# A mixture-of-experts kernel on one core: experts ranked by their token count, three of the eight passes in fp32 column tiles, one pass for 160 tokens

## The reference, cut to what matters

```python
N_EXPERTS = 8; TOP_K = 2; EXPERT_DIM = 3584            # D_MODEL = 1024, 256 tokens
logits = (xf @ router_w).astype(jnp.float32)
top_val, top_idx = lax.top_k(logits, TOP_K)
gates = jax.nn.softmax(top_val, axis=-1)
...
def expert_block(args):
    tok_b, e = args
    return swiglu(x_pad[tok_b], w1[e], w3[e], w2[e])    # (silu(x w1) * (x w3)) w2
```

## Time and profile before

| what | value |
|---|---|
| median of three runs | 1640.24 us |
| profiled execution, first to last instruction (its span; no other time of that execution is given) | 1635.5 us |
| median less span | 4.7 us |
| TensorE busy | 1608.7 us, 98% of the span |
| VectorE busy | 1425.0 us, 87% |
| ScalarE busy | 1163.9 us, 71% |
| GpSimd busy | 69.7 us, 4% |
| DMA | 520.04 MB, mean 318 GB/s |
| weights of the experts | 189 slots of 2 MB: 168 issued by SyncE, 21 by ScalarE |
| mean granted TensorE clock | 0.999 |

### The profile page before, as it was taken

One profiled execution on the slowest core, in us unless ns is written; L12 is line 12 of the kernel. 1 busy time (PEld: TensorE's weight loads), 2 busy tenths in 40 slices (PEclk: granted clock), 3 DMA queues, 4 the chain that ended last, 5 costly groups with the idle time before them and its releaser, 6 DMA issues.

```text
span 1635.5 us, 21435 instructions
## 1 busy us (share of the span) xinstructions
PE 1608.7 (98%) x8554; PEld 1361.2 (83%) x8554; DVE 1425.0 (87%) x1628; ACT 1163.9 (71%) x1427; POOL 69.7 (4%) x53
## 2 busy tenths in 40 slices
PE   6999999999999999999999999999999999999998
PEld 4867899998897888888888888888888888888887
DVE  2579888888766999999998999998999998999997
ACT  3567544446556877888887888887888887888885
POOL 0000000000000000200200200200200200200200
PEclk9999999999999999999999999999999999999999
DMA  9956768877812998999998999999999999999992
GB/s 351 331 211 236 252 254 299 302 268 290 289 73 104 351 354 332 354 376 377 352 380 335 353 376 377 355 369 345 352 378 372 354 368 349 354 367 359 373 366 83
DMA packets 170323, 520.04 MB, mean 318 GB/s; under 512 B 6861, under 2 KB 9050, under 8 KB 170218
## 3 DMA queue, kind: packets, MB, share of 16 engines
q1 hardware_dynamic: 156736, 473.32, 77.5%
q10 hardware_dynamic: 13482, 45.29, 7.3%
HBM read 516.50 MB, written 2.10 MB: 317 GB/s over the span
## 4 chain that ended last, share of the span: by engine, by line
PE 81%; DVE 12%; DMA 3%; ACT 2%; issue 1%; ACTq 0%; DVEq 0%
PE bank L1335 20%; PE bank L1339 20%; PE bank L1338 20%; DVE ada_acc L1999 4%; DVE w_lo L2200 3%; DMA ring<-in_ffn_w 3%; PE bank L809 2%; PE bank L1349 2%; PE bank L772 2%; PE bank L766 2%; PE bank L1072 1%; PE bank L1266 1%; DVE w_lo L2491 1%; PE bank L1074 1%; PE bank L1075 1%
## 5 line engine op out<-in xcount | busy, mean ns | idle before, releaser
L2491 DVE TENSOR_TENSOR w_lo<-ring,w_hi 128x1024 fp32r<-128x1024 f32 x756 | 928.6, 1262 | 59.8 <-ACT w_hi L1801 37.4
L1801 ACT ACTIVATE w_hi<-ring 128x1024 fp32r<-128x1024 f32 x756 | 799.8, 1063 | 193.7 <-PE bank L1339 191.5
L1335 PE MATMUL bank<-w_hi,hg_hi 128*128 128x512 f32 x1008 | 394.0, 391 | 0.7 <-DVE hg_lo L2504 0.6
L1339 PE MATMUL bank<-w_hi,hg_lo 128*128 128x512 f32 x1008 | 392.5, 389 | 0.0
L1338 PE MATMUL bank<-w_lo,hg_hi 128*128 128x512 f32 x1008 | 392.3, 389 | 0.0
L1335 PEld LDWEIGHTS bank<-w_hi,hg_hi 128*128 128x128 f32 x1008 | 189.3, 188 | 40.2 <-DVE w_lo L2491 1.2
L1339 PEld LDWEIGHTS bank<-w_hi,hg_lo 128*128 128x128 f32 x1008 | 189.2, 188 | 39.4
L1338 PEld LDWEIGHTS bank<-w_lo,hg_hi 128*128 128x128 f32 x1008 | 189.3, 188 | 38.3
L1335 PE MATMUL bank<-w_hi,hid_hi 128*128 128x512 f32 x496 | 195.6, 394 | 0.0
L1339 PE MATMUL bank<-w_hi,hid_lo 128*128 128x512 f32 x496 | 193.4, 390 | 0.0
L1338 PE MATMUL bank<-w_lo,hid_hi 128*128 128x512 f32 x496 | 193.2, 389 | 0.0
(11 more groups left out here) (398 smaller groups left out, 2063.4 us busy)
## 6 DMA issues: line engine op xcount, KB each, us to landing
ring<-in_moe_w SPq DMA_DIRECT2D x168, 2048.0 KB, 8.2
ring<-in_ada_w SPq DMA_DIRECT2D x24, 2048.0 KB, 12.8
ring<-in_moe_w ACTq DMA_DIRECT2D x21, 2048.0 KB, 9.8
ring<-in_ffn_w SPq DMA_DIRECT2D x15, 2048.0 KB, 8.3
ring<-in_gla_w_in SPq DMA_DIRECT2D x6, 2048.0 KB, 12.8
ring<-in_da_w_in SPq DMA_DIRECT2D x4, 2048.0 KB, 12.5
ring<-in_da_w_in SPq DMA_DIRECT2D x4, 1024.0 KB, 17.2
ring<-in_da_w_out SPq DMA_DIRECT2D x2, 2048.0 KB, 10.6
```

Of the source, the lines that this page charges most:

```text
L1335: begun = mm(out[:, :], xhi, whi[:, cs], start=first, stop=False)
L1339: last = mm(out[:, :], xlo, whi[:, cs], start=False, stop=end)
L1801: A(w_hi[:, moe_slot(Q), :], raw_piece(m, q), ACT.Copy).then_inc(hi_done, 1)
L2491: v.tensor_tensor(w_lo[:, moe_slot(Q), :], raw_piece(m, q), w_hi[:, moe_slot(Q), :].bitcast(F32), ALU.subtract).then_inc(lo_done, 1)
```

## The change

**Ranking.** In pass 0, which always takes expert 0, VectorE ranks experts 1 to 7 by token count (`places`) and writes the expert of each later pass into `ovi`. SyncE reads these seven numbers into registers, one for each slot it issues from slot 14 of pass 0 on, and loads the weights of passes 1 to 7 from addresses given by register. Gates and positions are put in the order of the passes (`gate_m`, `pos_m`).

**Kinds of passes.** The eight passes have the kinds A B A A A B C B. By `PLACES`, pass 6 gets the expert with most tokens of the seven, passes 2, 3 and 4 ranks 1 to 3, passes 1, 5 and 7 ranks 4 to 6.

- A, 128 slots: as before.
- B, 64 slots (`light`): no splitting. The moving operand is the weight slot itself in fp32, the stationary operand 128x64 tokens in fp32 (`xb`). Two column groups of 64 work on the two halves of a slot's columns, so a slot takes 8 matmuls of 512 columns (16 of 256 in the last chunk), and a result of 64 tokens by 1024 columns lies in one bank. ScalarE and VectorE do only the SiLU, the product, the copies and the gather. A slot is released by its last matmul. The first pieces of the pass that follows are split only after the light pass's last step on ScalarE and VectorE.
- C, 128 + 32 slots: 128 tokens as in A; the further 32 in plain fp32 in four column groups of 32 (`further_up` after each w1 slot, using it and the w3 slot behind it, which is ordered next to it; `further_down` after each w2 slot), with their own transposes, gates and scatter.

**Overflow.** Passes for experts whose tokens exceed the capacity of their pass run after the end of all eight, behind branches only (`overflow`). The ninth pass is no longer begun in any case, and ScalarE issues no slots unless a branch is taken.

**The end.** Pass 7 is a light one; `out_end` waits for its last slot, scales both halves (64 partitions each), splits, scatters and adds. `last_by_halves` is gone.

The core of the diff:

```diff
+BASE = "ABAAABCB"
+KINDS = BASE + "A" * OVER
+PLACES = (NE - 1, 4, 1, 2, 3, 5, 0, 6)
+CAPS = {"A": P, "B": HALF, "C": P + XT}          # 128, 64, 160
...
-                    src, k, n = expert_source(m, i)
+                    src, k, n = expert_source(ids[m], KINDS[m], i)
                     sp.dma_start(slot_view(at, k, n), src).then_inc(landed[at % SLOTS], 16)
+                    if m == 0 and i >= PER - NE + 1:
+                        j = len(ids)
+                        sp.wait_ge(s_places, 1)
+                        ids.append(sp.value_load(ovi[0:1, j:j + 1], min_val=0, max_val=NE - 1))
...
+            def further_up(m, c, part):
...
+                for kk in range(n):
+                    k = 4 * part + kk
+                    for g in range(4):
+                        w = slot_view(at[g // 2], n, width)
+                        last = mm(psum[4][XT * g:XT * (g + 1), 0:hw], xc[:, k, :], w[:, kk, g % 2 * hw:(g % 2 + 1) * hw],
+                                  start=(k == 0), stop=(k == KT - 1))
+                last.then_inc(slot_left, 1)
...
+            def further_down(m, c, part):
...
+                for p in range(PPC):
...
+                    for half in range(2):
+                        g = 2 * half + p % 2
+                        last = mm(psum[5][XT * g:XT * (g + 1), :], hidx[:, c % 2, j, XT * h:XT * (h + 1)],
+                                  w[:, p, half * 512:(half + 1) * 512], ...)
...
+            def light(m):                                     # on TensorE
+                for i in range(PER):
...
+                    wait_landed(pe, at)
+                    if what == "w2":
...
+                            for half in range(2):
+                                last = mm(psum[2][half * HALF:(half + 1) * HALF, :], x, w[:, p, half * 512:(half + 1) * 512], ...)
+                    else:
...
+                            for h in range(2):
+                                last = mm(psum[0 if what == "w1" else 6][h * HALF:(h + 1) * HALF, 0:hw], xb[:, k, :],
+                                          w[:, kk, h * hw:(h + 1) * hw], start=(k == 0), stop=(k == KT - 1))
+                    last.then_inc(slot_left, 1)
+                    if i == 1:
+                        spread(m - 1, "B")
...
-            expert(NE - 1)
-            expert(NE, 0, HEAD)
+            for m in range(NE):
+                if m == MORE_IN:
+                    pe.wait_ge(s_ovf, 1)
+                    more = [pe.value_load(...) for o in range(OVER)]
+                if KINDS[m] == "B":
+                    light(m)
+                else:
+                    expert(m)
+            spread_end()
             with pe.If(more[0] == 2):
-                expert(NE, HEAD, EQ - PPC)
-                last_by_halves(NE)
+                overflow(0)
```

More of the change, by code:

```diff
@@ new lines, in spread, with gates_of @@
+                    if kind == "C":
+                        mm(out, PmTX[rows, tokens], hid_1[0][rows, 1, 0:512], start=False, stop=False)
+                        last = mm(out, PmTX[rows, tokens], hid_1[1][rows, 1, 0:512], start=False, stop=True)
+                    last.then_inc(s_sct, 1)
+            def gates_of(m, tt):
+                if m == 0:
+                    return gate[:, tt, 0:1]
+                if m < NE:
+                    return gate_m[:, tt, m:m + 1]
+                return gate_o[:, tt, m - NE:m - NE + 1]
@@ L1292, in expert, with further_turned @@
+            def further_turned(m, c):
+                pe.wait_ge(s_xr, c + 1)
+                bank = psum[6 if c else 5]
+                for j in range(own_width(c) // P):
+                    last = nc.tensor.transpose(bank[:, j * P:(j + 1) * P], xraw[:, j * P:(j + 1) * P], ident[:])
+                last.then_inc(s_xtr, 1)
+            def expert(m):
+                kind = KINDS[m]
+                hosts = 0 < m < NE
+                for q in range(EQ):
                     i, p = divmod(q, PPC)
-                    what, c, part = eorder[i]
+                    what, c, part = orders[kind][i]
@@ L1340, in expert @@
                     last.then_inc(w_free, 1)
+                    if kind == "C" and p == PPC - 1 and what == "w1":
+                        further_up(m, c, part)
+                    if kind == "C" and p == PPC - 1 and what == "w2":
+                        further_down(m, c, part)
                     if q in TURN_AT:
@@ L1868, in store_end, with overflow @@
+            def overflow(o):
+                m = NE + o
+                for i in range(SLOTS):
+                    load_over(over[o], m, i)
+                gathered(group_of(m))
+                expert(m, over)
+                high_out(m)
+                act.wait_ge(s_scb, 4 * out_no(m) + 4)
             def store_end():
@@ L1949, in _ @@
+            store_end()
         @block.vector
@@ new lines, in overflow @@
+            def overflow(o):
+                m = NE + o
+                dve.wait_ge(s_gg, m)
+                dve.wait_ge(s_add_end, 4)
+                dispatch(m)
+                gathered(group_of(m))
+                expert(m)
+                raw_out(m)
+                low_out(m)
+                for n in range(4):
+                    tt, half = divmod(n, 2)
+                    dve.wait_ge(s_sct, 4 * out_no(m) + n + 1)
+                    dst = x_acc[:, tt, half * 512:(half + 1) * 512]
+                    v.tensor_tensor(dst, dst, psum[2 + n][:, :], ALU.add).then_inc(s_scb, 1)
+                dve.wait_ge(s_scb, 4 * out_no(m) + 4)
@@ L2635, in _ @@
+            split_to(piece_no(0, 0), 0)
+            gathered(0)
+            for m in range(NE):
+                if m == MORE_IN:
+                    dve.wait_ge(s_ovf, 1)
+                    more = [dve.value_load(ovi[0:1, NE + o:NE + o + 1], min_val=1, max_val=2) for o in range(OVER)]
+                if KINDS[m] == "B":
+                    light(m)
+                else:
+                    expert(m)
+            out_end()
             with dve.If(more[0] == 2):
-                expert(NE, over, HEAD, EQ)
+                overflow(0)
```

774 lines of the change are left out of this document (484 added, 290 removed).

## The result

The kernel with the change takes 1489.68 us, the median of 4 runs (1489.12 to 1491.39). The kernel before, run beside it, takes 1639.62 us (1638.48 to 1641.15). The ratio is 0.9087, with a 95% interval of 0.9074 to 0.9100: faster. The prediction was 1490 us, with a range of 1465 to 1535. The profiled execution took 1489.15 us with a span of 1487.4 at a granted clock of 0.995; the prediction had a span of 1485.2.

The account below looks back on a forecast made before the run. TensorE was taken to bound the kernel, DMA the light passes. Trunk 527.4, pass 0 129.1, three B 276, three A 365.1, C 164.5, transitions 14.6, end 8.5: span 1485.2, 150.3 less; median 1490 us, range 1465 to 1535.

Parts of the forecast that it names:

- The ninth pass and the trunk: No branch taken, so the ninth pass goes, worth 122 us; first expert matmul stays at 527.4 us.
- A light pass on TensorE: Two 64-column tiles overlap fully: 3.45 us a slot, 72 us for 21 slots, 80 to 85 with transposes, scatter and stalls.
- partial overlap: Rival in light passes: two tiles overlap only partly, 4.35 us a slot, 1515 us in all; chance 0.06.
- DMA bounds it: Light passes wait for weights: 16.4 slots at 5.4 us plus the last slot's matmuls, 92 us instead of 121.7.
- After a light pass: Before passes 2 and 6 TensorE idles 4.3 us, plus 3 each for missing lead and late transfers; 14.6 total.
- Passes 2 to 4: Three A passes at 121.7 us each, 365.1 together; restart loss before pass 2 counted separately.
- Pass C: Pass 6 adds `further_up` 24.2, `further_down` 12.1, transposes 1.9 and more to an A pass: 164.5 us.
- The changes of width: In pass C, switching matmul tile width costs 0.11 us, 28 times, 3 us.
- C stalls: Rival in pass C: its waits come in sequence, not covered; C 195 to 200, time 1525 us; chance 0.09.
- Pass 0: `places` and the larger table add small chained VectorE steps; 4 us charged, pass 0 129.1 us.
- The end: From the last matmul through scalings, splits, additions and store: 8.5 us against 7.7, +0.8.
- The clock as a rival: In light passes the clock falls, costing 5 to 15 us each, 1520 us (1664 if all at 1.2 GHz); chance 0.07.

Follow-up runs that it names:

- e4: Against the change, light-pass loads bring only the first half of each slot's k blocks, same matmuls, light experts' results wrong; 1448.0 us.
- e10: Against the change, both column halves of light passes go to one column group (PSUM partitions 0 to 63), results wrong; 1663.1 us.
- e11: Against the change, the ring has 5 slots in place of 6 everywhere; 1567.0 us.
- e5: Against the change, three spare fp32 matmuls on TensorE behind each light pass, two behind the last; 1487.1 us.
- e2: Against the change, pass 6 is of kind A, so the expert with 155 tokens overflows into a pass behind the branch; 1593.9 us.
- e8: Against the change, `further_up` in pass C does a quarter of its matmuls, result of the 32 further slots wrong; 1470.7 us.
- e6: Against the change, pass 0's overflow table moves to piece 82 (was 48), positions and gates to piece 40 (was 28); 1485.9 us.
- e9: Against the change with spare matmuls after light passes and late tables (1482.3 us), SyncE issues the four final stores instead of ScalarE; 1483.4 us.

## Why the prediction was right, step by step

*The ninth pass and the trunk.* No branch was taken and 168 slots came. The first expert matmul is at 528.8, 1.4 us later than assumed.

*A light pass on TensorE*: 3.45 us a slot predicted, 3.5 measured; 78.4 us a pass (e4) against 80 to 85. That two tiles of 64 would overlap as four of 32 do was taken from the earlier trace rows, and e10 shows what it is worth: 173 us. The rival "partial overlap" did not come about: it asks for 4.35 us a slot.

*DMA bounds it*: right in the mechanism (e4, e11), and 2.8 us too long in size: 89.2, 89.1 and 90.7 us instead of 92. The mis-sized term is the pitch of delivery, 5.4 us, for which I took the 387 GB/s of the earlier trace rows. The stretches at 660, 696 and 738 move 407 to 410 GB/s, 5.12 us a slot; only the last chunk's slots, whose rows are half as long, run at 387 (the stretch from 720). Over light pass 1 it is 403, 5.2 us: 16.4 x 5.2 + 3.65 = 88.9. The row that I picked, the stretch from 35 in the kernel before, was itself one of short rows: it has 974 packets for 1.93 MB, 2 KB each, where 738 to 744 has 620 for 2.46 MB, 4 KB each. Over three passes this gave 7 us.

*After a light pass*: idle 3.7 us against 4.3. The loss behind it, put at 3 us for a missing lead and late transfers, is 1.6 at both restarts (e4), from two causes. In pass C it is the clock alone, which I had not named for this place: with the clock kept (e5) the pass is as short as in e4. In passes 2 to 4 the clock kept gives back 0.3, and 1.4 remain (370.4 for the 369.0 of e4): TensorE waits for splits, and ScalarE 1.9 us for two slots. There the missing lead and the late transfers cost nearly as much without the clock's fall. That term was right in kind, and about half as dear.

*Passes 2 to 4*: 370.6 us against 368.1. The period of 121.7 from the earlier trace rows is a mean over passes of 120.0 and 123.9 in turn, those of 123.9 with a gather; two of these three have one: 367.8, and 1.6 behind the restart. The other 1.2 stay open; they are there in e4 too (369.0).

*Pass C*: 170.2 us against 167.5 (164.5 and the restart's 3). `further_up` 25.5 for 24.2, `further_down` 13.5 for 12.1, transposes 2.2 for 1.9; against the same pass as A (e2, 125.2 us) C costs 45.0 for the 42.8 of the sum. The changes of width that were charged apart are inside these. ScalarE's wait cost nothing, as e8 has it: 18.0 us out of the matmuls, 18.0 out of the pass. "C stalls" is thereby out.

*Pass 0*: 129.7 us against 129.1; the charge of 4 us for the small steps is the 3.8 that e6 took back.

*The end*: 11.5 us against 8.5, the largest miss of a single term. The clock is a small part: the scatter's matmuls are 0.63 long at 0.50 of the clock, and the last addition ends 6.0 us after the last expert matmul (5.4 predicted; 5.6 with the clock kept, e5). The rest is the store, from the kernel after:

```profile
1479.07 2.82 DVE L2872 TENSOR_TENSOR rstd<-rstd,bank 128x512 f32<-128x512 f32 x4
...
1479.91 3.03 ACTq L2167 DMA_DIRECT2D out_x<-rstd  x4
1480.11 0.63 PE L1585 MATMUL bank<-hid_hi,PmT 64*128 64x512 f32 x1
```

The additions end at 1481.89 and the span at 1487.4: 5.5 us where the earlier trace rows gave 3.1. The last issue ends 1.1 us after the additions (0.4 in the kernel before), and its store lands 4.1 us later (1.8 before).

*The clock as a rival* was half right. Inside the light passes, busy for 61 to 73% of the stretches from 720 to 750 with gaps of about 1.5 us, the granted clock stays at 1.00. It fell where I had not put it: after the 3.7 us of idle TensorE at each restart, and after the 2.4 us behind the last light pass. The Trainium skill, "TensorE: Matmul & The Clock Gate", section "HAM oscillation — how this bites in real kernels", tells of a kernel of thin matmuls that lost the clock in each of its DMA waits of some 3 to 5 us; the trace here agrees for the idle 3.7 us, and the shorter gaps inside the light passes cost none.

In sum the terms were off by +1.4 (trunk), +0.6 (pass 0), -6.8 (light passes), -1.2 (idle), +2.5 (passes 2 to 4), +2.7 (C) and +3.0 (end): +2.2 us in the span. The median stands 2.3 above this profiled span where I had used 4.7, and that took it back. The result at 0.3 us from the forecast is a sum of errors that cancel; the mechanism was right, but it does not earn that precision.

## What to carry to other kernels

When heavy passes are bound by an engine and light ones by transfers, alternate them over one ring: each light pass then begins with the slots that the heavy one saved, and each of those takes a delivery (5 us here) off it. Work out a light pass from the rate with the queue full and the row length that it will have, and look behind it: the first wait of the next heavy pass can be paid twice, once idle and once in clock. Matmuls that fill it won 1.6 us where the splits kept up with the faster start, and 0.3 where they did not. Small chained steps belong where their engine has nothing due, even if that is a pass later.

## What had not been expected of the hardware

- Two column groups overlap nearly as well when a whole half is issued before the other: a further slot takes 3.55 us against 3.43 alternating and 6.96 in one group, and each unbroken run of slots 1.9 to 2.0 us more.
- Rows of 2 KB move at 387 and rows of 4 KB at 410 GB/s, with the queue full in both.
- The last store of the output landed 4.1 us after its issue had ended, where the kernel before took 1.8, whichever engine issued it (e9). From 1484.5 us on, the queues of the kernel after were

```profile
q10 hardware_dynamic: 30, 0.03, 3.8%
q8 instruction: 1, 0.02, 2.1%
```

  and those of the kernel before, in its last 5.5 us:

```profile
q10 hardware_dynamic: 576, 1.05, 49.3%
```

  A packet of instruction loading falls beside the last store only in the kernel after. Whether it is the cause was not tried; it stays open.
- With five slots instead of six the trunk lost 63 us, in its waits for the SwiGLU weights; why so much was not tried.
